# Two-block transformer kernel: one root for two nested norms, output units in twos behind a norm, other places for the small work of VectorE

## What is computed

```
def _modulate(x, g, shift, scale):
    return _rmsnorm(x, g) * (1.0 + scale) + shift
# _mixer_out, first block
    y_g = _chunk_mlp(p[..., OFF_U:OFF_U + W_G], p[..., OFF_V:OFF_V + W_G], g_v, w_s, b_s)
    merged = gate_r * (y_r @ w_pr) + gate_g * (y_g @ w_pg)
    return merged @ w_out
def _conv_ffn(h, w_up, cw, cb, w_down, grid_h, grid_w):
    up = h @ w_up
    g = _dwconv2d(up[..., :D_FF].reshape(B, grid_h, grid_w, D_FF), cw, cb).reshape(B, T, D_FF)
    return (jax.nn.gelu(g) * up[..., D_FF:]) @ w_down
# end of the first block
    h2 = _modulate(x, g_norm2[l], m_x[:, 3], m_x[:, 4])
    x = x + m_x[:, 5] * _conv_ffn(h2, w_up[l], ffn_conv_w[l], ffn_conv_b[l], w_down[l], rows, GRID_W)
    return _rmsnorm(x, g_final)
# second block
    h = rms_norm(x, mix_norm_g[layer])
    u, q, k, v, f_logit, g_ssm, g_att = jnp.split(h @ w_in[layer], IN_SPLITS, axis=-1)
    y_ssm = s5_branch(u, ...)
    h2 = rms_norm(x, ffn_norm_g[layer])
    x = x + peer_ffn(h2, peer_w_query[layer], ...)
```

## Time and profile before

| | us |
|---|---|
| median of 3 runs | 3511.77 |
| the 3 runs | 3507.78, 3511.77, 3512.67 |
| profiled execution, its own time | 3513.08 |
| span of its trace | 3510.8 |
| PE busy (share of the span) | 3349.7 (95%) |
| DVE busy | 2020.5 (58%) |
| ACT busy | 1074.9 (31%) |
| POOL busy | 428.6 (12%) |

### The profile page before, as it was taken

How to read it: one execution, slowest core, us unless ns; L and a number is a source line. 1 busy time by engine, 2 the same in 40 slices (tenths; PEclk the granted TensorE clock), 3 DMA queues, 4 the chain that set the end, 5 groups by cost and what they waited for, 6 DMA issues and landing times.

```text
span 3510.8 us, 37934 instructions
## 1 busy us (share of the span) xinstructions
PE 3349.7 (95%) x14700; PEld 2622.5 (75%) x14700; DVE 2020.5 (58%) x3751; ACT 1074.9 (31%) x1394; POOL 428.6 (12%) x184
## 2 busy tenths in 40 slices
PE   7999898999999968999989999999999999999999
PEld 6866677876878745676567888888888788888887
DVE  4656624346798779934643758666651155555554
ACT  2145422223323222123523323355552211111111
POOL 0000000002314000000000344422324200000000
PEclk6988899999999989999999999999999999999999
DMA  5124322332233333222012344467877555555553
GB/s 183 37 90 123 105 84 91 116 123 66 85 120 113 103 110 104 93 73 78 30 60 90 103 138 139 140 152 190 194 189 218 171 192 184 188 192 185 187 192 114
DMA packets 280946, 451.56 MB, mean 129 GB/s; under 512 B 147776, under 2 KB 154048, under 8 KB 280512
## 3 DMA queue, kind: packets, MB, share of 16 engines
q1 hardware_dynamic: 145152, 405.10, 35.0%
q10 hardware_dynamic: 135616, 44.04, 5.9%
HBM read 369.39 MB, written 79.69 MB: 128 GB/s over the span
## 4 chain that ended last, share of the span: by engine, by line
PE 86%; DVE 10%; ACT 2%; issue 1%; DMA 0%; ACTq 0%; DVEq 0%
PE psum L571 86%; DVE wl L1289 1%; DVE ht L1685 1%; ACT wh L912 1%; DVE lb L1486 1%; DVE st L1694 0%; DVE n L1437 0%; DVE trig L1383 0%; DVE yb L1495 0%; DVE y L1490 0%; DVE trig L1384 0%; DVE trig L1386 0%; DVE trigw L1385 0%; DVE trigw L1382 0%; DVE trig L1381 0%
## 5 line engine op out<-in xcount | busy, mean ns | idle before, releaser
L571 PE MATMUL psum<-h_hi,wh 128*128 128x512 f32 x2144 | 871.1, 406 | 51.4 <-DVE h_lo L1431 20.8
L1289 DVE TENSOR_TENSOR wl<-ring,wh 128x1024 fp32r<-128x1024 f32 (+2 forms) x320 | 375.7, 1177 | 919.2 <-ACT wh L912 918.9
L571 PE MATMUL psum<-h_lo,wh 128*128 128x512 f32 x2144 | 851.8, 397 | 0.0
L571 PE MATMUL psum<-h_hi,wl 128*128 128x512 f32 x2144 | 849.2, 396 | 0.0
L912 ACT ACTIVATE wh<-ring 128x1024 fp32r<-128x1024 f32 (+2 forms) x492 | 504.3, 1027 | 897.8 <-PE psum L571 840.4
L1944 POOL TENSOR_TENSOR wl<-ring,wh 128x1024 fp32r<-128x1024 f32 x172 | 425.0, 2472 | 2000.4 <-ACT wh L912 2000.4
L571 PEld LDWEIGHTS psum<-h_hi,wh 128*128 128x128 f32 x2144 | 405.6, 189 | 157.7 <-issue 42.0
L571 PEld LDWEIGHTS psum<-h_hi,wl 128*128 128x128 f32 x2144 | 405.8, 189 | 101.7
L571 PEld LDWEIGHTS psum<-h_lo,wh 128*128 128x128 f32 x2144 | 406.5, 190 | 91.2 <-issue 4.1
L571 PE MATMUL psum<-ews_hi,wh 128*128 128x512 f32 x1024 | 408.7, 399 | 0.7 <-ACT ga L1259 0.7
L571 PE MATMUL psum<-ews_hi,wl 128*128 128x512 f32 x1024 | 403.5, 394 | 0.0
(11 more groups left out here) (357 smaller groups left out, 3917.9 us busy)
## 6 DMA issues: line engine op xcount, KB each, us to landing
ring<-tables SPq DMA_DIRECT2D x256, 512.0 KB, 3.7
acts_scratch<-ga SPq DMA_DIRECT2D x128, 256.0 KB, 2.2
gates_scratch<-stage ACTq DMA_DIRECT2D x8, 4096.0 KB, 27.2
abuf<-acts_scratch SPq DMA_DIRECT2D x128, 256.0 KB, 3.9
gbuf<-gates_scratch SPq DMA_DIRECT2D x128, 256.0 KB, 4.1
ring<-w_up SPq DMA_DIRECT2D x44, 512.0 KB, 3.6
ring<-w_modb SPq DMA_DIRECT2D x32, 512.0 KB, 3.6
statew<-states_scratch SPq DMA_DIRECT2D x16, 640.0 KB, 3.8
```

The lines of the kernel that those rows point to most:

```text
L571: return nc.tensor.matmul(out, lhsT, rhs, start=first, stop=last, **kw)
L1289: TT(wl, slot(t, 0, size[t]), wh.bitcast(F32), ALU.subtract).then_inc(S("low_by_ve"), 1)
```

## The change

1. `project_two` takes two units at once: per chunk three matmuls for the one and three for the other, both units marked done at the end. It is used for g0 and g1, u2_0 and u2_1, query0 and query1.
2. Norm 1: the raw tile is x times scale times the reciprocal in one operation; the shift is added by ACT in the high part's copy and by DVE in the rest's. All norms use three raw buffers and not four.
3. Nested norms: mean((x g r1)^2) + eps under the second root is written out, so that one root and one reciprocal give r1 times r2 from bank 6 + eps times bank 5 (with eps squared as the bias). r1 alone is a second root on ACT; its reciprocal stands behind norm 2 on DVE.
4. `input_map(0)` stands ahead of the eight yg tiles.
5. Tables: beside down0 the steps are dealt out otherwise, k = 8 in four quarters. Batch 2 is built beside l16 to l19, down1_0 and down1_1, batch 3 beside down1_2 to down1_5. Beside a down unit the add to x now stands ahead of the table steps. ACT parks batch 2 at down1_3 and batch 3 at down1_7.
6. `states_out` writes to banks 7 and 4 in turn and waits for the read of the fourth step before; `skip` stands ahead of `turned`.
7. ACT waits for x_normed in the first two head steps and not ahead of the loop. One operation at the start computes eps squared.

```diff
--- before.py
+++ after.py
@@ -596,6 +597,18 @@
...
+            def project_two(names, act, ready, at):
+
+                for name in names:
+                    block_free(pe, BLOCK[name])
+                    halves_here(pe, HALF[TILE[name]])
+                for k in range(KD):
+                    pe.wait_ge(S(ready), at + k + 1)
+                    lasts = [three(bank(BLOCK[name]), whl(HALF[TILE[name]], k), act, k, k == 0, k == KD - 1)
+                             for name in names]
+                lasts[0].then_inc(PE, 1)
+                lasts[1].then_inc(PE, 1)
...
@@ -717,7 +730,8 @@
...
-            for name in FFN:
+            project_two(("g0", "g1"), h, "norm_done", KD)
+            for name in FFN[2:]:
...
@@ -725,9 +739,10 @@
...
-                    project(name, h, ready="norm_done" if name == "g0" else None, at=KD)
-            for n in range(KS):
-                project(f"u2_{n}", h, ready="norm_done" if n == 0 else None, at=2 * KD)
+                    project(name, h)
+            project_two(("u2_0", "u2_1"), h, "norm_done", 2 * KD)
+            for n in range(2, KS):
+                project(f"u2_{n}", h)
...
@@ -742,10 +757,10 @@
...
             def states_out(c):
                 if c % 4 == 0:
-                    wait(pe, S("ys_read"), c // 4)
+                    wait(pe, S("ys_read"), c // 4 - 1)
                 for k, part in enumerate((0, 2, 1, 3)):
                     pe.wait_ge(S("turned"), 4 * c + k + 1)
-                    last = mm(psum[:, 7, :], outw[:, c % 3, part // 2 * P:(part // 2 + 1) * P], turned[:, part, :],
+                    last = mm(psum[:, (7, 4)[c // 4 % 2], :], outw[:, c % 3, part // 2 * P:(part // 2 + 1) * P], turned[:, part, :],
...
@@ -830,8 +845,9 @@
...
-            for n in range(16):
-                project(f"query{n}", h, ready="norm_done" if n == 0 else None, at=3 * KD)
+            project_two(("query0", "query1"), h, "norm_done", 3 * KD)
+            for n in range(2, 16):
+                project(f"query{n}", h)
...
@@ -1048,9 +1064,9 @@
...
-                    raw = nrm[k][(4, 5, 0, 1)[c % 4]]
+                    raw = nrm[k][(4, 0, 1)[c % 3]]
                     if scale is None:
-                        A(h[0][:, c, :], raw, ACT.Copy).then_inc(S("h_high"), 1)
+                        A(h[0][:, c, :], raw, ACT.Identity, bias=mod[:, 24 + c, 0:1]).then_inc(S("h_high"), 1)
...
@@ -1099,8 +1115,12 @@
...
-                    if n == 5:
-                        park_table(2 * int(name[4]))
+                    if name == "down0_5":
+                        park_table(0)
+                    if name == "down1_3":
+                        park_table(2)
+                    if name == "down1_7":
+                        park_table(3)
...
@@ -1108,10 +1128,9 @@
...
-            root(2, 4 * KD)
             act.wait_ge(S("second_sum"), 2)
-            A(nrm[2][2], nrm[2][0], ACT.Sqrt, scale=1.0 / D, bias=epsc).then_inc(S("sd_done"), 1)
-            park_table(3)
+            A(nrm[2][2], nrm[2][4], ACT.Sqrt, scale=1.0 / D, bias=eps_sq).then_inc(S("sd_done"), 1)
+            A(nrm[2][5], psum[:, 5, :], ACT.Sqrt, scale=1.0 / D, bias=epsc).then_inc(S("sd_done"), 1)
...
@@ -1140,6 +1159,8 @@
...
+                else:
+                    act.wait_ge(S("x_normed"), KD)
...
@@ -1423,21 +1444,24 @@
...
-                raws = [nrm[k][j] for j in (4, 5, 0, 1)]
+                raws = [nrm[k][j] for j in (4, 0, 1)]
 
                 def rest(c):
                     ve.wait_ge(S("h_high"), k * KD + c + 1)
                     if shift is None:
-                        ins = STT(h[1][:, c, :], raws[c % 4], scale[:, c:c + 1], h[0][:, c, :].bitcast(F32),
+                        ins = STT(h[1][:, c, :], raws[c % 3], scale[:, c:c + 1], h[0][:, c, :].bitcast(F32),
                                   ALU.mult, ALU.subtract)
                     else:
-                        ins = TT(h[1][:, c, :], raws[c % 4], h[0][:, c, :].bitcast(F32), ALU.subtract)
+                        ins = STT(h[1][:, c, :], raws[c % 3], shift[:, c, 0:1], h[0][:, c, :].bitcast(F32),
+                                  ALU.add, ALU.subtract)
                     ins.then_inc(S("norm_done"), 1)
                 for c in range(KD):
-                    ins = TT(raws[c % 4], x[:, c, :], rstd, ALU.mult)
-                    if shift is not None:
-                        link(ins)
-                        ins = TS(raws[c % 4], raws[c % 4], scale[:, c:c + 1], shift[:, c, 0:1], ALU.mult, ALU.add)
+                    if c >= 3:
+                        ve.wait_ge(S("norm_done"), k * KD + c - 2)
+                    if shift is None:
+                        ins = TT(raws[c % 3], x[:, c, :], rstd, ALU.mult)
+                    else:
+                        ins = STT(raws[c % 3], x[:, c, :], scale[:, c:c + 1], rstd, ALU.mult, ALU.mult)
...
@@ -1564,8 +1561,37 @@
...
+            ve.wait_ge(S("yr_ready"), NR)
+            ve.wait_ge(S("bsrow_loaded"), 16)
+            input_map(0)
+            for hd in range(HG):
+                b = BLOCK["mix"] + hd
...
             for n in range(KD):
-                input_map(2 * n)
+                if n:
+                    input_map(2 * n)
...
@@ -1606,8 +1632,15 @@
...
-            turns = [(0, 0, 4), (1, 0, 4), (2, 0, 4), (3, 0, 4)], [(4, 0, 4), (5, 0, 4), (6, 0, 4)], [(7, 0, 4)], \
-                [(8, 0, 2), (8, 2, 4)]
+            small_steps = [(0, 0, 4), (1, 0, 4), (2, 0, 4), (3, 0, 4), (4, 0, 4)]
+            turns = small_steps, [(5, 0, 4), (6, 0, 4)], [(7, 0, 4), (8, 0, 1)], [(8, 1, 2), (8, 2, 3), (8, 3, 4)]
+            angles_at = {f"down0_{n}": (n // 4, turns[n % 4]) for n in range(KD)}
+            for n, steps in enumerate((small_steps[:3], small_steps[3:], [(5, 0, 4)], [(6, 0, 4)])):
+                angles_at[f"l{16 + n}"] = 2, steps
+            angles_at["down1_0"] = 2, [(7, 0, 4)]
+            angles_at["down1_1"] = 2, [(8, 0, 2), (8, 2, 4)]
+            for n in range(4):
+                angles_at[f"down1_{n + 2}"] = 3, turns[n]
...
@@ -1641,25 +1674,26 @@
...
                     half = int(name[4])
-                    if half and n % 4 == 0:
-                        ve.wait_ge(S(f"tables_parked{n // 4}"), 16)
-                    for k, lo, hi in turns[n % 4]:
-                        angles(2 * half + n // 4, k, lo, hi)
-                    if n % 4 == 3:
+                    add_to_x(f"down{half}_", n, "x_ffn", mod_t[:, 2 * n + 80:2 * n + 81])
+                if name in angles_at:
+                    batch, steps = angles_at[name]
+                    if batch >= 2 and steps[0][0] == 0:
+                        ve.wait_ge(S(f"tables_parked{batch % 2}"), 16)
+                    for k, lo, hi in steps:
+                        angles(batch, k, lo, hi)
+                    if steps[-1] in ((8, 3, 4), (8, 2, 4)):
                         ve.sem_inc(S("table_ready"), 1)
-                    add_to_x(f"down{half}_", n, "x_ffn", mod_t[:, 2 * n + 80:2 * n + 81])
             ve.wait_ge(S("x_ffn"), 2 * KD)
-            r1, r13, work = nrm[2][3], nrm[2][4], nrm[2][0]
+            second, r1, rstd = nrm[2][4], nrm[2][5], nrm[2][3]
+            ve.wait_ge(S("sq_used"), 4 * KD)
+            TS(second, psum[:, 5, :], EPS, None, ALU.mult).then_inc(S("second_sum"), 1)
+            ve.wait_ge(S("second_sum"), 1)
+            TT(second, second, psum[:, 6, :], ALU.add).then_inc(S("second_sum"), 1)
             ve.wait_ge(S("sd_done"), 3)
-            link(v.reciprocal(r1, nrm[2][2]))
-            TT(work, psum[:, 6, :], r1, ALU.mult).then_inc(S("second_sum"), 1)
-            ve.wait_ge(S("second_sum"), 1)
-            TT(work, work, r1, ALU.mult).then_inc(S("second_sum"), 1)
+            link(v.reciprocal(rstd, nrm[2][2]))
+            norm(2, 3, gm, None, rstd)
             ve.wait_ge(S("sd_done"), 4)
-            link(v.reciprocal(r13, nrm[2][2]))
-            rstd = nrm[2][2]
-            link(TT(rstd, r13, r1, ALU.mult))
-            norm(2, 4, gm, None, rstd)
+            link(v.reciprocal(r1, r1))
...
@@ -1669,7 +1703,7 @@
...
-                STT(ysk, u2[:, oc, :], C("dskip", oc), psum[:, 7, :], ALU.mult, ALU.add).then_inc(S("ys_read"), 1)
+                STT(ysk, u2[:, oc, :], C("dskip", oc), psum[:, (7, 4)[oc % 2], :], ALU.mult, ALU.add).then_inc(S("ys_read"), 1)
...
@@ -1705,6 +1739,8 @@
...
                 wait(ve, S("out_done"), c)
+                if c % 4 == 0 and c:
+                    skip(c // 4 - 1)
                 ve.wait_ge(step, 4 * c + 3)
                 TT(turned[:, 0, :], st[:, 1, :], cc, ALU.mult).then_inc(S("turned"), 1)
                 STT(turned[:, 2, :], st[:, 1, :], -1.0, ss, ALU.mult, ALU.mult).then_inc(S("turned"), 1)
@@ -1713,8 +1749,6 @@
                     head_norm(c - 2)
-                if c % 4 == 0 and c:
-                    skip(c // 4 - 1)
                 if c % 4 == 1 and c > 1:
                     halve(c // 4 - 1)
             low_after(TILE[BESIDE[NS - 1]])

```

33 lines of the change are left out of this document (17 added, 16 removed).

## The result

| | median us | range | against before, ratio (95% interval) |
|---|---|---|---|
| before | 3512.22 | 3507.78 to 3512.96 | |
| changed kernel | 3487.80 | 3482.99 to 3488.65 | 0.9931 (0.9919 to 0.9943) |
| the same, in a later session | 3485.80 | 3483.55 to 3488.16 | 0.9928 (0.9914 to 0.9942) |

The change took 24.4 us off; 32 were forecast, and 3487.8 lies near the upper end of 3474 to 3489. The profiled execution of the changed kernel has a span of 3486.1 us, 24.7 less than before. Where the 7 us went can't be read from the total, only stage by stage.

A forecast was written before the change was run, and what follows sets the result against it. PE, busy 95% of the span, was taken as the bound, so gains lay in its waits. Terms 6.2 + 1.2 + 14.5 + 4.7 + 2.3 + 0.8 + 2.3 = 32.0 gave 3480 us against 3511.77, range 3474 to 3489.

The forecast's parts named there:

- the map's remaining wait: Ahead of gg0: PE's wait of 11.43 us becomes one of about 5, with 6.2 us gained.
- the wait at l13: Ahead of l13's matmuls: PE, 6 to 8 us ahead, waits 4 to 6 for POOL's low part.
- the steps at l16 to l19: Batch 2's table steps, 11.6 us in DVE's idle time there: 0 gained, or a loss of 0 to 8.
- down1's sum: Down1 to its last sum of squares: ends at 1236.2 instead of 1251.02, 14.5 us gained (10 to 15.5).
- The clock behind a wait: Behind each long PE wait: seven to nine matmuls at 1.2 GHz, 0.2 us each, costing 1.4 to 1.8 us.
- The term of 1.2: Norm 1, g0 and g1 through l13: 1.2 us gained of 6 (0 to 4 in the forecast).
- Swallowed at l13: Norm 1 to l13: PE's 6 us lead doesn't last; it waits 4 to 6 at l13, then 1.6 for the clock.
- u2 and state loop: Pair u2_0, u2_1 gains 2.3 us (0.5 to 3); second bank in the state loop gains 0.8 (-1 to 2.5).
- the rival "less": l16 to l21: DVE late, PE stands for a bank or ffs_lo; 5 to 10 us less, about 3488; chance 0.16.
- More: At l13: low part isn't late, norm 1's 6 us stay; 5 to 7 us more, 3474; chance 0.12.
- The clock: Pairs stay at 1.2 GHz to their end: 7.9 us less at u2 and query; about 3497; chance 0.04.
- Slower: l13, l16 to l19: POOL holds DVE at nearly every table step; 42 lost against 32, 3522; chance 0.02.

The follow-up runs named there:

- the kernel with the fold back: Changed kernel with norm 1 again in three operations a chunk (product, scale and shift, rest), pairs and three raw buffers kept: 3487.8 us, ratio 0.9936.
- the run with three improvements: Changed kernel with k = 8 in halves (batch 1's second half at l12, l13), gg0's low part earlier, down1_7's add before low parts: 3478.45 us.

## Why the prediction came out as it did

**Right in sign and range, and in the large terms.** Down1 to its last sum was forecast at 81 us and took 81.3, the nested norms at 8.1 and took 8.08, the map's remaining wait at 5 and was 4.42, the wait at l13 at 4 to 6 and was 6.01; the steps at l16 to l19 cost nothing. Down1's cause was right too: the add behind the steps. I put the loss down to the squares' wait alone; it is 3.5 us now and was 12.1, and with the add behind the steps at their new places the loss comes through ScalarE's high parts instead. That batch 3's end would run into norm 2 without its new place is right as well (11.8 us waited, not 8.1). Two slips stand in down1's sum: 1251.02 - 1236.2 is 14.8, not 14.5, and the parts behind the last unit's matmuls add up to 9.7 to 11.6 with squares of 2.5, not 8.6 to 10.5. They took 9.3.

**Too optimistic by 7.3 us** (32.0 against the 24.7 of the profiled executions).

- *The clock behind a wait*, 1.4 to 1.6 in the sums, from seven to nine matmuls. In the trace of before it already lasted for 6 to 11. Here it cost 2.8 at the map (24 matmuls of gg0 in 8.5 us, 5.7 at full clock), 2.2 at u2 (24.6 for 22.4) and 2.2 behind l13 (384 matmuls in 91.9 us for 89.7). Some 0.5 at the map and 0.8 at u2 of the missing gain are this. query0 gave 1.5 and not 2.3, for which I didn't separate the cause; the low clock lasted there for 10 matmuls, and for 11 before.
- *DVE beside down0.* The step "the convolution starts 0 to 1.5 earlier" left out that POOL, moved along with PE, could meet more table steps. There were five such and not four (2.1 us), and counted from norm 1's last sum the convolution started 0.7 later. Why one more was met is only argued. The term of 1.2 came out as -0.9. Undoing the quarters gave 3.8 back, moving k = 8 away 8.3.
- *Norm 1.* "Swallowed at l13" is right: 7.5 us won up to the end of down0 (0.8, 5.0 and 1.7), 8.3 lost behind it.
- *u2 and state loop*, 2.3 and 0.8 forecast. From u2_0 to vv 0.8 are there in all (354.07 and 353.27). The steps that failed are the assumption that the two gains add up, and that a lead of DVE at the loop's start lasts: DVE sets the pace for three quarters of it, then it waits 1.31 us for PE and the pair's 1.5 are gone. The run with one bank and the run with single units took the same time as both together (353.21 and 353.22). No run takes both out of the changed kernel at once, so what gives the 0.8 stays open.
- *A stage that the change doesn't touch.* vv lost 2.7 us. The same 96 matmuls behind the same wait of 3.15 us, before and after, in the window's row (from:to, us, busy of PE, PEld, DVE, ACT, POOL, clock, DMA share, GB/s):

```profile
1618.00:1640.60 22.60, 22.59 (x97) 18.19 (x98) 3.67 (x3) 3.18 (x3) 0.00 (x0) 1.00 0.31 103
```

```profile
1593.30:1618.50 25.20, 25.20 (x96) 20.16 (x97) 3.68 (x3) 3.19 (x3) 0.00 (x0) 0.88 0.29 90
```

The granted clock is 1.00 before and 0.88 after. In the kernel with the fold back it was 0.94 (23.9 us). 1.2 us came back between the scores and query0 in the same way; in other runs that stretch took up to 208.2 (205.1 in the changed kernel). What sets which of these a kernel gets stays open; it repeated when the kernel was run again, and it changed between kernels with the same code in front. No step of mine allowed for it, and the chance of the rival "less" should have held it: such stages move a total by some 3 us either way, and the start by up to 6.

**The rivals.** *Less* came nearest in its number (3488) and not by its mechanism: PE stood for neither bank nor ffs_lo between l16 and down1_0. *More* failed, since the wait at l13 came. *The clock* didn't come: 12 of the 48 matmuls ran at the low clock at g0, 10 at u2_0 and 10 at query0, a little more than assumed. *Slower* didn't come, but the run with three improvements shows its mechanism: with eleven meetings 7.1 us of waits for POOL and 2.2 for ffs_lo.

## What to carry to other kernels

Taking work off the path before a stage in which another engine is already late gives nothing until that engine's backlog is moved too: here eight us returned only when table steps left the place beside down0. Likewise a gain at one place counts only when it is still there behind the next stage: the 1.5 us of the pair at u2 were gone by vv. Small VectorE steps with two SBUF inputs are cheap filler only where POOL rests; beside POOL one of 0.17 us cost 2.40 here, a whole POOL operation, and which steps are hit shifted with the changes ahead. Where kernels differ by some us of 3500, compare stages between the same two instructions, not medians, and look at how long the low clock lasts in each before giving a difference of 1 or 2 us to an edit.

## What the runs showed that I had not expected

- A VectorE operation on 128x8 elements took 2.40 us instead of 0.17 beside a POOL operation, and the one behind it 2.41, since POOL had a second operation queued.
- The same wait of 3.15 us ahead of the same 96 matmuls was followed by a granted clock of 1.00, 0.94 or 0.88, 22.6 to 25.3 us, according to the kernel; and the same 2.75 us ahead of the out units by 2.7 or 6.1 us of low clock, with the same code in front.
- The pair of u2_0 and u2_1 brought the state loop's start 1.5 us forward and vv not at all.
- The same work up to gr0 took from 558.6 to 564.6 us. Part of it was there early: a wait of 15.1 us for PE ended at 93.5 in the kernels before and after, at 90.5 in the run with the fold back.
